# Shift and scale weights loaded as eight row blocks, with the head columns and the small loads moved behind them

## The reference, cut to what matters

```
mod = jax.nn.silu(c) @ w['w_mod'] + w['b_mod']
sh1, sc1, gt1, sh2, sc2, gt2 = [m[:, None, :] for m in jnp.split(mod, 6, axis=-1)]
h = rms_norm(x, w['g_norm1']) * (1 + sc1) + sh1
proj = h @ w['w_in']
q, k, v, fl, z, xbc, dtr, ga, gb = split_cols(proj, IN_SIZES)
q = rms_norm(q.reshape(b, l, N_HEADS, HEAD_DIM), w['g_q'])
k = rms_norm(k.reshape(b, l, N_KV_HEADS, HEAD_DIM), w['g_k'])
logf = jax.nn.log_sigmoid(fl.astype(jnp.float32) + w['b_f'].astype(jnp.float32))
```

## Time and profile before

| | us |
|---|---|
| median of 3 runs | 771.57 |
| lowest and highest | 770.38, 772.34 |
| the profiled execution | 770.76 |
| span of its trace | 769.2 |

### The profile page before, as it was taken

The page is one execution under the profiler, slowest core; times in us unless marked ns, Lnnn a source line. Parts: engine busy times, 40 slices in busy tenths (PEclk is TensorE's granted clock), DMA queues, the critical chain, the costliest instruction groups (busy, mean ns, idle before and its releaser), DMA issues.

```text
span 769.2 us, 12251 instructions
## 1 busy us (share of the span) xinstructions
PE 727.5 (95%) x4419; PEld 499.0 (65%) x4419; DVE 382.6 (50%) x963; ACT 285.0 (37%) x670; POOL 99.2 (13%) x169
## 2 busy tenths in 40 slices
PE   3899998999999989999989989999999999999987
PEld 3475687778785668788868878887634344434434
DVE  1364337777674088798999211112423343324324
ACT  3221157656775123668885000012513122212201
POOL 4331021122110113620100100000010000000000
PEclk9999999999999999999999989999999999999999
DMA  9997364979786621359999595567899999999992
GB/s 316 331 344 227 116 205 153 331 232 322 241 300 186 216 60 57 114 158 390 365 318 333 197 397 203 163 259 296 320 411 422 416 421 422 416 421 421 419 413 80
DMA packets 90126, 219.46 MB, mean 285 GB/s; under 512 B 12982, under 2 KB 57238, under 8 KB 76622
## 3 DMA queue, kind: packets, MB, share of 16 engines
q1 hardware_dynamic: 73360, 181.71, 64.3%
q0 software_dynamic: 7840, 31.67, 12.1%
q10 hardware_dynamic: 8862, 5.25, 2.3%
HBM read 207.07 MB, written 13.22 MB: 286 GB/s over the span
## 4 chain that ended last, share of the span: by engine, by line
PE 56%; SPq 12%; DMA 9%; DVE 9%; ACT 6%; issue 4%; POOL 2%; POOLq 1%; ACTq 1%; DVEq 0%
PE bank L1786 15%; PE bank L2023 8%; SPq L599 8%; PE bank L2115 6%; PE bank L2031 4%; PE bank L2140 4%; SPq L597 3%; PE bank L1779 3%; PE bank L2007 3%; DMA conv_out<-in_w_mod 3%; DMA arena<-in_w_up 3%; PE bank L1696 3%; PE bank L1736 2%; DMA arena<-in_state_ssm 2%; DVE arena L1473 2%
## 5 line engine op out<-in xcount | busy, mean ns | idle before, releaser
L1786 PE MATMUL bank<-h_normed,weight_ring 128*128 128x264 f32 x1024 | 239.0, 390 | 3.2 <-ACT conv_work L1091 3.2
L1786 PEld LDWEIGHTS bank<-h_normed,weight_ring 128*128 128x128 f32 x1024 | 192.1, 191 | 39.1 <-issue 4.2
L2023 PE MATMUL bank<-y_T,weight_ring 128*128 128x264 f32 x256 | 60.6, 400 | 2.5 <-DVE y_T L1510 2.5
L2115 PE MATMUL bank<-arena,h_normed 128*64 128x512 f32 x136 | 60.3, 594 | 0.0
L2023 PEld LDWEIGHTS bank<-y_T,weight_ring 128*128 128x128 f32 x256 | 50.4, 198 | 11.7 <-issue 2.6
L1596 DVE TENSOR_TENSOR arena<-arena,bank 128x512 f32<-128x512 f32 x8 | 8.4, 1052 | 84.6 <-PE bank L2115 84.6
L1696 PE MATMUL bank<-identity,arena 128*128 128x128 f32 (+5 forms) x218 | 30.4, 281 | 14.0 <-ACT arena L904 9.8
L1083 ACT ACTIVATE arena<-conv_out,early_small 128x128 f32<-128x128 f32 x128 | 38.3, 387 | 11.1 <-DVE arena L1473 10.4
L873 POOL DMA_INDIRECT h_normed<-h_scratch,token_rows x7 | 7.1, 1020 | 252.6 <-DVE token_rows L1563 135.1
L2140 PE MATMUL bank<-arena 128*64 128x512 f32 x88 | 39.2, 595 | 0.0
L1395 DVE SCALAR_TENSOR_TENSOR conv_work<-conv_work,conv_out 128x288 f32<-128x288 f32 x72 | 37.7, 524 | 2.5
(11 more groups left out here) (404 smaller groups left out, 1212.0 us busy)
## 6 DMA issues: line engine op xcount, KB each, us to landing
weight_ring<-in_w_in SPq DMA_DIRECT2D x36, 1024.0 KB, 6.2
weight_ring<-in_w_mod SPq DMA_DIRECT2D x22, 1024.0 KB, 10.2
arena<-in_w_down SPq DMA_DIRECT2D x11, 1024.0 KB, 23.8
arena<-in_w_gate SPq DMA_DIRECT2D x10, 1024.0 KB, 13.8
weight_ring<-in_w_down SPq DMA_DIRECT2D x10, 1024.0 KB, 14.4
weight_ring<-in_w_up SPq DMA_DIRECT2D x9, 1024.0 KB, 24.9
arena<-in_state_ssm POOLq DMA_DIRECT2D x8, 1024.0 KB, 11.2
out_ssm_sample<-arena POOLq DMA_DIRECT2D x8, 1024.0 KB, 8.5
```

The lines of the kernel that those rows point to most:

```text
L1786: ins = mm(ps[:, 0:T], w, hT[:, c, :], start=c == 0, stop=c == KD - 1)
L2023: ins = mm(ps[:, 0:T], w, yT[:, c, :], start=c == 0, stop=c == NXB - 1)
L2115: ins = mm(banks[i][BLK * e:BLK * e + BLK, :], xg[:, 4 * h + c, BLK * e:BLK * e + BLK], ws[e][c], start=h == 0 and c == 0, stop=h == 1 and ...
```

## The change

- The shift and scale weights come as eight blocks of 128 rows by 2048 columns: one piece of 8 KB for each partition. The job `mc` multiplies one block into `sbank` as soon as it has landed; the eight of them stand between the flips of x, `ssq` and `vecs`. The result is there after the last block, for shift and scale together.
- ACT copies it in two halves (`condrow`), `mt 0` and `mt 1` flip a half each. `ssq`'s 1/rms is multiplied into `hT` for all tokens beforehand, while blocks arrive. After each `mt`, DVE makes the gains of four chunks, finishes their samples and two of the chunks (`modulated`), ACT finishes the other two. The first `k` job takes the chunks in the order 0, 4, 1, 5, 2, 6, 3, 7 and waits for each.
- Eight matmuls on x between the blocks go; three stand behind `mt 1`.
- `cst` moves behind `q 0`, `fd` from ahead of `k` to behind the first query norms (`qb 0` to `3`), `ft` from behind `q 0` to behind `v 2`, `qn 1` to behind `ft`.
- SP issues the head columns behind three blocks of `w_in`; the first blocks of `w_in` wait for the `mc` jobs that free their places. ACT issues the convolution states and the nine head vectors after `mt 1`. POOL waits for `k 0` before the cached log-forget values.

```
-        jobs += [("vecs",), ("mod", 1), ("ssq", 0), ("modt", 1), ("mod", 0), ("modt", 0), ("cst", 0), ("cst", 1), ("fd",)]
-        jobs += [("k", i) for i in range(4)] + [("q", 0), ("ft",), ("q", 1), ("kn", 0), ("q", 2)]
+        jobs += [("mc", 7), ("mt", 0), ("mt", 1)] + [("k", i) for i in range(4)] + [("q", 0), ("cst", 0), ("cst", 1), ("kn", 0), ("q", 1)]
+        jobs += [("qb", i) for i in range(4)] + [("fd",), ("q", 6), ("q", 7), ("v", 0), ("v", 1), ("v", 2), ("ft",), ("qn", 1)]
...
-                if s == ("in", COL_K):
+                if s == ("in", SW):
                     load_small()
...
+                if before[s] and before[s][0] == "cond":
+                    sp.wait_ge(cond_used, before[s][1] + 1)
...
+                if s[0] == "cond":
+                    sp.dma_start(dst, wmod[:, s[1]:s[1] + 1, 0:2 * D]).then_inc(slot_full[r], 16)
...
-            bk, use = bank_of[("mod", 0)]
+            bk, use = bank_of[("k", 0)]
             pool.wait_ge(bank_filled[bk], use)
+            with pool.Fori(0, NS) as b:
+                for q in range(NPG):
+                    pool.dma_start(lfc[:, q, bass.ds(b * NH, NH)], clf[page(b * NPG + q)]).then_inc(lf_in, 16)
...
+                elif k == "mc":
+                    if j[1] == KD - 1:
+                        act.wait_ge(cond_used, KD)
+                        for h in range(2):
+                            fn(condrow[:, 256 * h:256 * h + 256], sbank[:, 256 * h:256 * h + 256], ACT.Copy).then_inc(cond_rows, 1)
+                elif k == "mt":
+                    act.wait_ge(gsc_ready, j[1] + 1)
+                    for c in (2 * j[1], 2 * j[1] + 1):
+                        fn(hT[:, c, 0:NP], hT[:, c, 0:NP], ACT.Identity, scale=gsc[:, c, NS:NC], bias=modT[:, c, NS:NC])\
+                            .then_inc(h_low, 1)
+                    if j[1]:
+                        act.dma_start(csin, t["state_conv"].rearrange("o b w (q c) -> (o b w q) c", q=4)).then_inc(st_in, 16)
...
+            def modulated(h):
+                def both(x):
+                    return x.rearrange("p (x y) n -> p x y n", x=2)[:, :, 2 * h:2 * h + 2, :]
+                for x in range(2):
+                    ks = slice(4 * x + 2 * h, 4 * x + 2 * h + 2)
+                    ins = v.scalar_tensor_tensor(gsc[:, ks, :], modT[:, KD + ks.start:KD + ks.stop, :], 1.0,
+                                                 vec[:, 48 + ks.start:48 + ks.stop].unsqueeze(2).to_broadcast([128, 2, NC]),
+                                                 ALU.add, ALU.mult)
+                link(ins, gsc_ready)
+                hs = both(hT[:, :, NP:T])
+                link(v.tensor_tensor(hs, hs, both(gsc[:, :, 0:NS]), ALU.mult))
+                link(v.tensor_tensor(hs, hs, both(modT[:, 0:KD, 0:NS]), ALU.add))
+                for c in (4 + 2 * h, 5 + 2 * h):
+                    v.tensor_scalar(hT[:, c, 0:NP], hT[:, c, 0:NP], gsc[:, c, NS:NC], modT[:, c, NS:NC], ALU.mult, ALU.add)\
+                     .then_inc(h_high, 1)
...
+                    link(v.tensor_tensor(hT[:], xT[:], rs[:, 0:1, :].to_broadcast([128, KD, T]), ALU.mult))
...
+                elif k == "mc":
+                    c = j[1]
+                    read_out(pe, ("cT",))
+                    landed(("cond", c))
+                    for i in range(4):
+                        ins = mm(sbank[32 * i:32 * i + 32, :], cT[:, c, :], slot(("cond", c))[:, 0, 512 * i:512 * i + 512],
+                                 start=c == 0, stop=c == KD - 1, tile_position=(0, 32 * i))
+                    ins.then_inc(cond_used, 1)
+                    continue
```

More of the change, by code:

```diff
@@ L318, in slots_of @@
             k = j[0]
+            if k == "mc":
+                return [("cond", j[1])]
             if k == "mod":
@@ L763, in page @@
                 return pool.value_load(pgs[0:1, bass.ds(i, 1)], min_val=0, max_val=ck.shape[0] - 1)
-            with pool.Fori(0, NS) as b:
-                for q in range(NPG):
-                    pool.dma_start(lfc[:, q, bass.ds(b * NH, NH)], clf[page(b * NPG + q)]).then_inc(lf_in, 16)
             def score_bias(c):
@@ L1128, in _ @@
                     act.wait_ge(sd_ready, 1)
-                    fn(sdiag, ident[0:NS, 0:NS], ACT.Copy, scale=rw[0][0:NS, 2:3]).then_inc(sdiag_ready, 1)
+                    fn(sdiag, ident[0:NS, 0:NS], ACT.Copy, scale=rw[0][0:NS, 2:3]).then_inc(sd_ready, 1)
                 elif k == "rk":
@@ L1724, in _ @@
                     ins = flip(ps[:, 104:200], vrow[0:96, 1, :])
+                elif k == "mc":
[7 more added lines that the diff above has]
+                    continue
+                elif k == "mt":
+                    pe.wait_ge(cond_rows, j[1] + 1)
+                    for q in range(2):
+                        ins = flip(ps[:, 128 * q:128 * q + 128], condrow[:, 256 * j[1] + 128 * q:256 * j[1] + 128 * q + 128])
+                    if j[1]:
+                        done(ins, j)
+                        for _ in range(3):
+                            mm(sbank[:, 0:T], xT[:, 0, 0:128], xT[:, 1, :], start=True, stop=True)
+                        continue
                 elif k == "mod":
-                    read_out(pe, ("cT",))
                     for c in range(KD):
                         s = ("mod", 4 * j[1] + c // 2)
-                        if j[1] == 0 and c in (2, 4, 6):
-                            read_out(pe, ("xt", 2, 1))
-                            for _ in range((3, 3, 2)[c // 2 - 1]):
-                                mm(sbank[:, 0:T], xT[:, 0, 0:128], xT[:, 1, :], start=True, stop=True)
                         if c % 2 == 0:
@@ L1774, in _ @@
                         landed(x)
-                    for c in range(KD):
+                    for c in (0, 4, 1, 5, 2, 6, 3, 7):
+                        if j == ("k", 0):
+                            pe.wait_ge(h_high, c % 4 + 1)
+                            if c < 4:
+                                pe.wait_ge(h_low, c + 1)
                         if k == "q":
```

92 lines of the change are left out of this document (43 added, 49 removed).

## The result

The changed kernel takes 776.16 us (median of 20 executions, 772.83 to 779.27), the kernel before beside it 771.99 (768.01 to 774.78): a ratio of 1.0056 (95% interval 1.0041 to 1.0070), 4.2 us slower. The forecast was 772.5 with a range up to 775.0. The sign was right, but the loss is four times the +1.0 us of the sum.

A forecast was written before the change was run, and what follows sets the result against it. Bound by DMA and the short chain behind the last block before the first matmul on `hT`, then by PE's work and new waits. Terms -2.8 + 0.7 + 0.66 + 2.4 = +1.0 us gave 772.5 us; 8-in-10 range 770.0 to 775.0.

The forecast's parts named there:

- part 3: Jobs changing place on PE: `fd` and `ft` cost the same, flips of `cst` behind `q 0` lose 0.66 us.
- Part 4: At `ft` beside `qn 1`: PE waits 2.4 us for DVE's square behind `ft`'s copies; lower bound 2.0.
- the head chain: Between `fd` and `ft`: 16.3 us of DVE and ACT work fits under five jobs of 18.2 us, no wait.
- Part 1: In the opening: the last shift and scale block lands 2.8 us earlier, bounds 1.2 to 3.4 us.
- States and head vectors: In the opening: moved loads gain 0.74 us for the states' bytes and 0.6 us for the first rate shortfall.
- Head columns: In the opening, 26 to 30 us: the rate shortfall when they come in, taken as a gain of 0.4 us.
- Pieces of 8 KB: Block loads in the opening: 422 against 400 GB/s gains 1.1 us; the skill's packet rule gave 0.2 us.
- The rival of a larger gain: Landing of the blocks: 422 GB/s from 3 us on gains about 4.5 us, giving 770.4 us; chance 0.12.
- Part 2: Chain behind the last block: 4.1 us where it was 3.66, plus 0.25 us wait; 0.7 us lost together.
- The clock rival: In the opening: PE falls to 1.2 GHz, adding 3 to 4.6 us, around 776.3 us; chance 0.14.
- wait for the K block: Rival ahead of `k 0`: the K block lands last, `k 0` starts at 34, 774 to 775 us; chance 0.09.
- its two rows: Clock evidence for the opening: PE busy 0.69 of 3.4 us, then half clock; 1.55 of 3.41 us kept 2.4 GHz.

The follow-up runs named there:

- e_knft: Changed kernel with `kn 0` moved behind `q 1` and `ft` behind `v 3`, covering both waits; 771.80 us, 1.0003 to the kernel before.
- a_again: The changed kernel itself, run again on one chip beside the kernel before; 777.31 us, ratio 1.0074.
- p_4k: f_early with each modulation block loaded as two pieces of 4 KB a row in place of one of 8 KB; ratio 1.0016.
- f_early: Changed kernel with jobs reordered so DVE has a projection job between each piece of its work and the waiting matmul; 770.05 us, 0.9970 to the kernel before.
- n_bare: Kernel before without its eight matmuls on x between the blocks, nothing else; 773.85 us, 1.0032 to the kernel before.
- h_gaps: f_early with one matmul on x ahead of block 5 and two ahead of block 7; 768.87 us, 0.9967 to the kernel before.
- q_three: f_early with states and head vectors issued ahead, head columns right behind the modulation blocks, and blocks in 4 KB pieces; 1.0049 to the kernel before.
- m_cols: f_early with the two head-column loads issued ahead of the first K block again; 0.9982 to the kernel before.
- f_again: f_early once more, beside h_gaps; 771.59 us, 0.9999 to the kernel before.

## Why the prediction was wrong, point by point

- **The step that failed is part 3.** It moved `cst` in between `q 0` and `kn 0` and counted PE's 0.66 us. DVE's copies behind those flips (1.33 us) were not counted, and `kn 0` stands right behind them. Part 4 worked out just that for `ft` and `qn 1`; the same question asked at every moved job would have found it. It cost 2.77 us, and 2.4 more in `q 1` where the clock fell with it; with both waits covered the loss is gone (e_knft, 1.0003 beside a_again's 1.0074).
- **Part 4 was right.** A wait of 2.4 us was forecast, 2.48 came, with the square behind `ft`'s copies as described. The norm behind it was even and the head chain fitted.
- **Part 1 was too small in sum and wrong in a term.** The landing gained 3.7 us, 0.3 above the upper bound. States and head vectors: 0.74 + 0.6 forecast, 1.5 measured. Head columns: 0.4 and 0.3. Pieces of 8 KB: 1.1 forecast, 0.2 measured. The Trainium skill, "DMA: Bandwidth & Descriptors", section "Why small descriptors are slow (HBM only)", had given 0.2 by the estimate in the prediction, and p_4k agrees with it (27.56 to 27.75 us). The row of the experts' 422 GB/s was of a stage in which hardly anything but expert weights was loading. The rival of a larger gain was added up wrongly: blocks in by 25.5 us, against 30.9, would be a gain of 5.4 and not 4.5 us.
- **Part 2 was right at the high clock:** 4.1 us forecast, 27.33 to 31.45, 4.12 us in f_early. At the low clock it is 6.1, since the three matmuls on x (2.85 us) run past the gains, as the rival said.
- **The clock rival met the number partly by luck.** It gave 776.3 us, and 776.16 came. Its sign came too, 1.2 GHz near 28 us; but that cost some 2.0 us in the profile of the result, not 3 to 4.6, and nothing in a_again's, while it did not know the wait at `kn 0` and the fall behind it. On one chip at a clock of 0.990 the changed kernel stands 2.8 us above the kernel before (775.9 against 773.1, good to about 1 us). That agrees with the forecast's sum with the forgotten wait, less what part 1 gained more: 1.0 + 2.8 - 0.9 = 2.9. The other 3 us of the 6.0 there go with the lower mean clock, 0.9872 against 0.9929. A chance of 0.14 was too small for a change that removes the matmuls that hold the clock (n_bare) and forecasts a wait besides.
- **Not met:** the changed kernel did not wait for the K block; h_gaps (some 0.3 us) and q_three (some 1.7) did. The first score did not wait for its bias, ready at 106.9 us and first used at 113.1. So neither of the two things that were to show the forecast wrong came: it was wrong at a place where it had not looked.

## What to carry over

When a job moves in a list that all engines walk, write down for each engine what now stands between it and the next job that another engine waits for: a flip that costs PE 0.7 us carried 1.4 us of another engine's work and a 2.8 us wait. Price a wait on TensorE with the slow stretch that may follow it (here 2.8 us of waiting, and up to 2.5 us of low clock behind it), and before you take out matmuls that compute nothing, ask what they hold up. A filler must be shorter than its gap: with one and two matmuls ahead of blocks 5 and 7 the last block's matmuls start at 27.4 to 27.6 us, as without them; with 3, 2 and 3 at 29.8.

## What the runs showed of the hardware

- The clock fell to 1.2 GHz behind a stretch with PE busy 2.04 of 3.40 us in the changed kernel, and stayed at 2.4 GHz behind one with 1.55 of 3.41 us in the earlier trace rows. So the forecast's comparison of the opening with its two rows could not have decided.
- The spread of one kernel's executions goes with the granted clock: 772.8 us at a mean of 0.995, 779.3 at 0.983, nearly 1%.
- Rows of 4 KB and of 8 KB differ by 0.2 us over 8 MB, no more than the landing of f_early's own two profiles (27.33 and 27.56 us), while 288 KB of states with nine tiny vectors beside them cost 1.5 us.
- The two loads of the head columns (192 KB) held SP's queue: in m_cols, where they stand ahead of the first K block, issuing the second of them took SP 18.25 us; the block was issued at 24.3 us and landed at 33.5, in f_again at 12.3 and 31.4.
